# Loading the weights of the first expert pairs: down 0 issued without the wait for the gather, gate 2 loaded in two parts

## The chip, the cores and the metric

One core of a Trainium2 chip runs the kernel. The metric is the device time of one execution in microseconds (us), where less is better. One execution is also recorded by the hardware profiler; its trace is what the rows below are read from. Engines are named as the profile names them: PE is TensorE's matmuls, PEld its weight loads, DVE VectorE, ACT ScalarE, POOL GpSimd, SP SyncE. A "q" behind a name (SPq) is that engine's instruction queue, which waits on semaphores and issues DMAs.

## The reference

The reference is one inference step of a layer for 512 prompt rows and 64 sample rows of width 1024. First come three token mixers side by side (attention, a gated linear recurrence, a state-space scan), then a mixture of experts, then a last norm. The change touches only the start of the experts:

```python
def run_trunk(x, layer_params, g_final, past):
    ...
        mix, st = token_mixers(rmsnorm(h, lp['g_mix']), lp, layer_past)
        h = h + mix
        h = h + hier_moe(rmsnorm(h, lp['g_ffn']), ...)
    ...
def hier_moe(u, w_rg, b_rg, w_re, b_re, w_eg, w_eu, w_ed):
    ...
    def run_block(args):
        xb, e = args
        return (jax.nn.silu(xb @ w_eg[e]) * (xb @ w_eu[e])) @ w_ed[e]
```

Each of the 576 rows picks one of 4 groups, and in it 2 of 8 experts. An expert has three weight matrices in float32: gate and up (1024 x 512) and down (512 x 1024), 2 MB each. All 32 experts are computed, so 32 x 6 MB = 201 MB of weights are read in any case.

## The kernel before

The kernel is written out engine by engine: each engine has its own program, and semaphores order them. There is no scheduler; what stands first in an engine's program is issued first, and a wait holds up everything behind it on that engine.

The experts are worked through in 16 pairs. Pair i is experts i and i + 16, with 64 slots for rows each, so that a pair fills 128 partitions. For pair i:

- POOL issues a gather (an indirect DMA, in POOL's `expert_pair`) that fetches the pair's 128 rows of 4 KB from `u2d` in HBM into `xg`. Its landing counts in `xg_in`.
- PE turns the rows (`turn_rows`, 8 transposes), ACT and DVE copy them to `xT`.
- PE computes the gate product (`gate`, which calls `into`; 8 steps over the 1024 inputs, 2 experts each, and two PE instructions per float32 matmul, so 32 instructions), then the up product (`into` again, 32 instructions).
- ACT and DVE make silu(gate) * up, PE turns the result, and computes the down product (`down`, 32 instructions, in two halves of the columns). The end of the second half counts in `down_b`.
- PE later adds the result to the rows that it belongs to (`scatter`).

PE runs ahead: its `expert_pair(i)` does up i, turns the rows of pair i + 1, does gate i + 1, and then down i. So the order on PE at the start is gate 0, up 0, gate 1, down 0, up 1, gate 2, down 1, up 2, and so on.

The weights come by SP. `load(kind, i, first, second)` waits until the product that used the buffer before is done, and issues two DMAs of 2 MB, one per expert. There are two buffers for gate weights (`w_g[0]` for even pairs, `w_g[1]` for odd pairs), one for up (`w_u`), and one for down (`w_d`). So gate 2 must wait for the gate product of pair 0 (`gate_done`), up 1 for the up product of pair 0 (`up_done`), and down 1 for `down_b` of pair 0. Gate 0 is loaded during the mixers' last products; the rest starts when the last of these is done (`pj_full`). In the program of before, SP also waits for the first gather's landing before it issues down 0:

```python
            sp.wait_ge(S["xg_in"], 16)
            load("down", None, 0, EPAIRS)
            load("gate", 2, 2, 2 + EPAIRS, 0)
            load("up", 1, 1, 1 + EPAIRS)
            load("down", 1, 1, 1 + EPAIRS)
```

After this start, a loop issues up, gate and down of the pairs that follow, each with its wait. Below, "gate 2" or "down 1" means the weights, or the product, of that pair. The functions that the change touches:

Of the kernel before, what the change touches and what calls it, by code (L numbers as in the profile page):

```python
# [27 lines left out]
P = 128  # L28
# [6 lines left out]
KD = D // P  # L35
# [26 lines left out]
DE = D // 2  # L62
# [4 lines left out]
EPAIRS = NE // 2  # L67
# [216 lines left out]
def trunk_and_experts(nc, a, o):  # L284

    ctx = ExitStack()
    with ctx:
# [6 lines left out]
        def sem(name):  # L294
            return ctx.enter_context(nc.semaphore(name))
# [6 lines left out]
        def take(n):  # L302
            cut[0] += n
            assert cut[0] <= ARENA, cut[0]
            return cut[0] - n

        def at(off, *dims):
            n = 1
            for d in dims:
                n *= d  # L310
            v = arena[:, off:off + n]
            if len(dims) == 2:
                v = v.rearrange("p (a b) -> p a b", a=dims[0])
            if len(dims) == 3:
                v = v.rearrange("p (a b c) -> p a b c", a=dims[0], b=dims[1])
            return v

        def region(name, off, n, dt=F32R):

            return nc.alloc_sbuf_tensor_at(name, [P, n], dt, offset=arena_at + 4 * off)[:, :]
# [73 lines left out]
        first = region("first", cut[0], 2 * 2048, F32)  # L398
# [90 lines left out]
        rank, first, twice, place, col, side, is_over, div = (at(take(2 * NT), NT, 2) for _ in range(8))  # L489
# [14 lines left out]
        w_g = [at(wexp_off, 2 * KD, DE), at(take(2 * KD * DE), 2 * KD, DE)]  # L504
# [71 lines left out]
        def last_bank(k):  # L576
# [10 lines left out]
            lru_mu lru_h ob_r hs_ps hs_r td_r dec_ps acs_r d_r ea_r em_r e_r m_r xdt_r xdd_r tz_r mix_ps  # L587
            hcd_r h_r y0_r y1_r y2_r yg_r ssy_r vy_r sy_r yn_r yt_ps oc_r so_ps so_r so_out v_out tl_out
            tl_ps tl_r gm_r gains_in u2_r u2t_ps u2t_r lg_ps lg_r ids_r fexp_in fexp_r idx_r idx_seen over_c xg_in
            xt2_ps xt2_a xt2_d wu_in wd_in gate_done up_done gate_th gate_mul hid_r hidt_ps hidt_r down_a  # L590
            down_b yh_r yl_r hot_r sc_ps sc_r over_ps over_r fin_r fin_out dve_c pool_c sp_dve sp_act lru_pool side_dma""".split()
        S = {n: sem(n) for n in names}
        x_in = [sem(f"x_in{t}") for t in range(NT)]
        wg_in = [sem(f"wg_in{s}") for s in range(2)]
# [40 lines left out]
        def _(sp):  # L635
# [13 lines left out]
            for u, unit in enumerate(UNITS):  # L649
# [25 lines left out]
                else:  # L675
                    w = a[{"in": "w_in", "gate": "w_gate", "out": "w_out"}[unit[0]]]
# [5 lines left out]
            def load(kind, i, first, second, turn=0):  # L682

                name, dst, used, before, arrived = {
                    "gate": ("w_expert_gate", w_g[turn], "gate_done", 2, wg_in[turn]),
                    "up": ("w_expert_up", w_u, "up_done", 1, S["wu_in"]),
                    "down": ("w_expert_down", w_d, "down_b", 1, S["wd_in"])}[kind]
                if i is not None:
                    sp.wait_ge(S[used], i - before + 1)
                k = (DE if kind == "down" else D) // P  # L690
                for j, w in enumerate((first, second)):
                    half = dst[:, k * j:k * (j + 1), :].rearrange("p k f -> p (k f)").unsqueeze(1)
                    sp.dma_start(half, expert_w(name, w)).then_inc(arrived, 16)

            def expert_w(name, e):

                return a[name][0].rearrange("e (p k) f -> p e (k f)", p=P)[:, bass.ds(e, 1), :]
# [8 lines left out]

            load("up", None, 0, EPAIRS)
            load("gate", None, 1, 1 + EPAIRS, 1)

            sp.wait_ge(S["xg_in"], 16)  # L710
            load("down", None, 0, EPAIRS)
            load("gate", 2, 2, 2 + EPAIRS, 0)
            load("up", 1, 1, 1 + EPAIRS)
            load("down", 1, 1, 1 + EPAIRS)
            with sp.Fori(1, EPAIRS // 2 - 1) as ii:
                for turn in range(2):
                    i = 2 * ii + turn
# [31 lines left out]
        def _(pe):  # L749
# [4 lines left out]
            def params(_):  # L754
                pe.wait_ge(S["consts"], 7)
                pe.wait_ge(S["par_in"], 16 * (len(PAR_ROWS) + 2))
                pe.wait_ge(S["par_up"], 1)
                pe.transpose(ms[:, 0:NPAR], st_a[0:NPAR, :], ident[0:NPAR, 0:NPAR])
                pe.transpose(oa[:, 0:NST], st_b[0:NST, :], ident[0:NST, 0:NST]).then_inc(S["pe_par"], 1)
# [106 lines left out]
            def dt_turn(_):  # L866
                wait_drained(pe, IDX[("dt", 0, 1)])
                pe.wait_ge(S["ko_r"], NT)
                for t, (o0, n) in enumerate(TT):
                    m = pe.transpose(ms[0:n, t * 8:t * 8 + 8], dtT[0:8, o0:o0 + n], ident[0:8, 0:8])  # L870
                m.then_inc(S["dt_ps"], 1)
# [85 lines left out]
            def state_in(_):  # L957
                pe.wait_ge(S["lruw_in"], 16 * 5)
                pe.wait_ge(S["dt_raw"], 1)
                for j in range(WT):  # L960
                    m = pe.transpose(ms[:, j * P:(j + 1) * P], ss_in[:, j, :], ident)
                m.then_inc(S["hs_ps"], 1)
# [173 lines left out]
            def turn_rows(i, spare):  # L1136

                pe.wait_ge(S["xg_in"], (i + 1) * 16)
                for k in range(KD):
                    z = oa if k < KD // 2 else ms  # L1140
                    m = pe.transpose(z[:, (k % 4) * P:(k % 4 + 1) * P],  # L1141
                                     xg.rearrange("s (p k) -> s k p", k=KD)[:, k, :], ident)
                m.then_inc(S["xt2_ps"], 1)

            def into(i, b, w, spare, done):

                for k in range(KD):
                    for j in range(2):
                        m = pe.matmul(za[j * BLK:(j + 1) * BLK, b, :], xT[spare][:, k, j * BLK:(j + 1) * BLK],  # L1149
                                      w[:, j * KD + k, :], start=k == 0, stop=k == KD - 1)  # L1150
                m.then_inc(S[done], 1)

            def gate(i, turn, spare):
                par, n_turn = turn
                pe.wait_ge(S["xt2_a"], i + 1)
                pe.wait_ge(S["xt2_d"], i + 1)
                pe.wait_ge(wg_in[par], (n_turn + 1) * 32)
                into(i, 0, w_g[par], spare, "gate_done")

            def down(i, q, ks):  # L1160
                for k in ks:
# [7 lines left out]
            def expert_pair(i, spare, ahead=None, behind=2, over=None, last=False):  # L1169

                pe.wait_ge(S["wu_in"], (i + 1) * 32)
                into(i, 1, w_u, spare, "up_done")
                if ahead is not None:
                    if behind > 0:
                        pe.wait_ge(S["hidt_r"], i)
                    turn_rows(i + 1, 1 - spare)
                if behind > 0:
                    scatter(i - 1, range(6), behind > 1)
                if ahead is not None:

                    pe.wait_ge(S["gate_mul"], i + 1)
                    gate(i + 1, ahead, 1 - spare)
                pe.wait_ge(S["hid_r"], i + 1)
                for k in range(DE // P):
                    m = pe.transpose(oa[:, k * P:(k + 1) * P],
                                     hid.rearrange("s (p k) -> s k p", k=DE // P)[:, k, :], ident)
                m.then_inc(S["hidt_ps"], 1)
                if behind > 0:
                    scatter(i - 1, range(6, 2 * NT))
                    pe.wait_ge(S["sc_r"], 2 * NT * (i - 1) + 8)  # L1190
                pe.wait_ge(S["hidt_r"], i + 1)
                pe.wait_ge(S["wd_in"], (i + 1) * 32)
                if behind > 0 or over is not None:
                    pe.wait_ge(S["yl_r"], 2 * i)
                down(i, 0, range(DE // P))
                if last:
                    down(i, 1, range(DE // P // 2))
                    scatter_last(range(NT))
                    down(i, 1, range(DE // P // 2, DE // P))
                else:  # L1200
                    down(i, 1, range(DE // P))
# [47 lines left out]
                    item(n)  # L1249
            pe.wait_ge(S["routed"], 2)  # L1250
            turn_rows(0, 0)
            gate(0, (0, 0), 0)
            expert_pair(0, 0, ahead=(1, 0), behind=0)
            expert_pair(1, 1, ahead=(0, 1), behind=1)
            pe.wait_ge(S["routed"], 3)
# [6 lines left out]
            with ExitStack() as more:  # L1262
                for j in range(OPAIRS):
                    more.enter_context(pe.If(total > j))
                    i = EPAIRS + j
# [12 lines left out]
        def _(act):  # L1278
# [43 lines left out]
            def params(_):  # L1322
                act.wait_ge(S["par_in"], 16 * (len(PAR_ROWS) + 2))
                act.activation(w_dt_hr, w_dt, ACT.Copy).then_inc(S["wdt_r"], 1)
                act.wait_ge(S["pe_par"], 2)
                act.wait_ge(S["ut_u"], NT)
                act.activation(cpar, ms[:, 0:NPAR], ACT.Copy).then_inc(S["par_up"], 1)
                act.activation(cst, oa[:, 0:NST], ACT.Copy).then_inc(S["par_up"], 1)
# [120 lines left out]
            def state_in(_):  # L1449
                act.wait_ge(S["hs_ps"], 1)  # L1450
                act.activation(hS, ms[:, :], ACT.Copy).then_inc(S["hs_r"], 1)
# [1135 lines left out]
```

## Time and profile before

| | us |
|---|---|
| median of 3 runs | 1218.59 |
| lowest and highest run | 1214.49, 1219.43 |
| the profiled execution's own time | 1217.82 |
| its span in the trace, first to last instruction | 1216.0 |

The profiled execution's own time holds 1.8 us that lie around the span. All times of day below are us from the span's start. The mixers, the output projection and the routing take the first 713 us; the first gather is issued at 713.4, and the last pair's up weights land at 1174.8.

### The profile page before, as it was taken

What the parts mean: (1) busy time and instruction counts of PE and PEld (TensorE: products, weight loads), DVE (VectorE), ACT (ScalarE), POOL (GpSimd) and SP (SyncE); (2) the same over time, 40 slices, a digit from 0 to 9 for tenths busy, and PEclk for the clock granted to TensorE, in tenths of its full rate; (3) what the DMA queues carried; (4) which work ended last, traced back from release to release, by engine and by line L of the source; (5) the groups of instructions that cost most, each with busy time, mean ns of one, the idle gap of its engine ahead of it and who ended that gap; (6) DMA issues with size and microseconds to landing.
All of it is one profiled execution on the core that took longest, in us unless ns stands there. A gap on an engine that the chain in (4) does not pass through costs nothing.

```text
span 1216.0 us, 17138 instructions
## 1 busy us (share of the span) xinstructions
PE 1126.3 (93%) x6833; PEld 803.8 (66%) x6833; DVE 528.4 (43%) x992; ACT 381.4 (31%) x600; POOL 181.6 (15%) x196
## 2 busy tenths in 40 slices
PE   4999999999999999999999869999999999999994
PEld 4898777777988899999999853443433334343432
DVE  4331767763246465543444541332333323232336
ACT  3323676565547444433431101110111101010103
POOL 4000100211313346542310010000000000000000
PEclk8999999998999999999999859999999999999998
DMA  8279544363322212225263198999999999999982
GB/s 184 74 129 112 45 53 42 47 52 37 61 65 63 78 54 71 61 78 158 87 208 128 64 371 356 426 427 428 427 429 427 427 428 426 430 427 427 428 346 80
DMA packets 94316, 263.16 MB, mean 216 GB/s; under 512 B 5021, under 2 KB 75897, under 8 KB 81961
## 3 DMA queue, kind: packets, MB, share of 16 engines
q1 hardware_dynamic: 87664, 250.36, 61.0%
q0 software_dynamic: 3456, 6.58, 1.5%
q10 hardware_dynamic: 3128, 5.29, 1.2%
q8 instruction: 46, 0.75, 0.3%
q14 instruction: 22, 0.17, 0.0%
HBM read 258.24 MB, written 7.64 MB: 219 GB/s over the span
## 4 chain that ended last, share of the span: by engine, by line
PE 57%; DMA 26%; DVE 8%; ACT 5%; issue 3%; SPq 1%; DVEq 0%; POOLq 0%
DMA arena<-in_w_expert_up 23%; PE za L1149 12%; PE pj L777 11%; PE pj L778 10%; PE pj L779 10%; PE pj L804 2%; DMA ring<-in_w_in 2%; PE zb L1163 2%; DVE arena L1870 1%; DVE arena L1831 1%; DVE arena L1832 1%; ACT arena L1421 1%; ACT arena L1417 1%; PE ms L1076 1%; DVE arena L1845 1%
## 5 line engine op out<-in xcount | busy, mean ns | idle before, releaser
L1149 PE MATMUL za<-arena 128*64 128x512 f32 x1024 | 234.7, 613 | 23.6 <-DMA arena<-in_w_expert_up 21.8
L777 PE MATMUL pj<-u_high_r,ring_r 128*128 128x288 f32 x736 | 224.7, 305 | 0.5 <-ACT arena L1339 0.5
L778 PE MATMUL pj<-u_rest_r,ring_r 128*128 128x288 f32 x736 | 217.3, 295 | 0.0
L779 PE MATMUL pj<-u_high_r,ring_r 128*128 128x288 f32 x736 | 217.3, 295 | 0.0
L1149 PEld LDWEIGHTS za<-arena 128*64 128x64 f32 x1024 | 73.7, 141 | 176.0 <-issue 141.2
L777 PEld LDWEIGHTS pj<-u_high_r,ring_r 128*128 128x128 f32 x736 | 138.7, 189 | 13.4 <-issue 10.2
L778 PEld LDWEIGHTS pj<-u_rest_r,ring_r 128*128 128x128 f32 x736 | 138.8, 189 | 0.6
L779 PEld LDWEIGHTS pj<-u_high_r,ring_r 128*128 128x128 f32 x736 | 138.6, 188 | 0.0
L1710 DVE TENSOR_TENSOR ring_r<-ring,ring_r 128x1024 fp32r<-128x1024 f32 x62 | 78.5, 1271 | 105.5 <-ACT ring_r L1306 105.4
L1163 PE MATMUL zb<-arena 128*64 128x512 f32 x512 | 113.6, 595 | 3.9 <-DMA arena<-in_w_expert_down 1.5
L1163 PEld LDWEIGHTS zb<-arena 128*64 128x64 f32 x512 | 36.1, 137 | 74.3 <-issue 71.5
L1306 ACT ACTIVATE ring_r<-ring 128x1024 fp32r<-128x1024 f32 x62 | 64.5, 1051 | 20.6 <-DMA ring<-in_w_in 17.4
L2232 DVE SCALAR_TENSOR_TENSOR arena<-arena,za 128x512 f32<-128x512 f32 x16 | 11.0, 688 | 119.0 <-PE za L1149 119.0
L2248 DVE SCALAR_TENSOR_TENSOR y_rest<-zb,arena,y_high 128x512 fp32r<-128x512 f32 x32 | 24.0, 750 | 89.0 <-ACT y_high L1586 89.0
L1586 ACT ACTIVATE y_high<-zb,arena 128x512 fp32r<-128x512 f32 x32 | 22.0, 687 | 127.5 <-PE zb L1163 127.5
L2538 POOL COPY arena<-arena 128x1 int32 (+1 forms) x15 | 2.7, 182 | 382.1 <-PE ms L1141 382.1
L777 PE MATMUL pj<-ring_r,u_high_r 128*128 128x256 f32 (+1 forms) x160 | 48.4, 303 | 11.5 <-ACT arena L1342 4.8
L1383 ACT ACTIVATE arena<-pj,arena 128x288 f32<-128x288 f32 x48 | 24.0, 500 | 107.0 <-PE pj L779 106.9
L2204 DVE TENSOR_TENSOR arena<-arena,pj 128x512 f32<-128x512 f32 (+1 forms) x90 | 57.1, 674 | 0.0
L1567 ACT ACTIVATE arena<-oa 128x512 f32<-128x512 f32 x16 | 9.6, 600 | 150.0 <-PE ms L1141 150.0
L1570 ACT ACTIVATE arena<-za 128x512 f32<-128x512 f32 x16 | 9.6, 598 | 145.7 <-PE za L1149 145.7
L2226 DVE SCALAR_TENSOR_TENSOR arena<-arena,za 128x512 f32<-128x512 f32 x16 | 11.0, 689 | 101.3 <-ACT arena L1570 101.3
(441 smaller groups left out, 2082.3 us busy)
## 6 DMA issues: line engine op xcount, KB each, us to landing
arena<-in_w_expert_gate SPq DMA_DIRECT2D x32, 2048.0 KB, 26.3
arena<-in_w_expert_up SPq DMA_DIRECT2D x32, 2048.0 KB, 17.6
arena<-in_w_expert_down SPq DMA_DIRECT2D x32, 2048.0 KB, 16.7
ring<-in_w_in SPq DMA_DIRECT2D x26, 512.0 KB, 9.1
ring<-in_w_gate SPq DMA_DIRECT2D x24, 512.0 KB, 4.3
arena<-in_x_prompt SPq DMA_DIRECT2D x8, 512.0 KB, 8.8
ring<-in_w_branch_out SPq DMA_DIRECT2D x8, 512.0 KB, 3.4
ring<-in_w_in SPq DMA_DIRECT2D x2, 1024.0 KB, 15.7
```

What stands on the lines that cost most here:

```text
L777: pe.matmul(out, left[0], right[0], start=k == 0, stop=False)
L778: pe.matmul(out, left[0], right[1], start=False, stop=False)
L779: return pe.matmul(out, left[1], right[0], start=False, stop=k == last - 1)
L804: m = pe.matmul(bank[:, 0:HALF], ring4[s][:, k, m_cols], oAT[:, k, cols], start=k == 0, stop=k == WT - 1)
L1149: m = pe.matmul(za[j * BLK:(j + 1) * BLK, b, :], xT[spare][:, k, j * BLK:(j + 1) * BLK], w[:, j * KD + k, :], start=k == 0, stop=k == KD - 1)
L1163: m = pe.matmul(zb[j * BLK:(j + 1) * BLK, q, :], hidT[:, k, j * BLK:(j + 1) * BLK], w_d[:, j * (DE // P) + k, q * 512:(q + 1) * 512], star ...
L1306: act.activation(high_r[s], raw[s], ACT.Copy).then_inc(S["high_r"], 1)
L1383: m = act.activation(gsb[k % 2], bank[:, 0:HALF], ACT.Tanh, scale=0.5, bias=cpar[:, j:j + 1])
L1586: act.activation(y_high[:, half], zb[:, q, :], ACT.Copy, scale=weight_now).then_inc(S["yh_r"], 1)
L1710: dve.tensor_tensor(rest_r[s], raw[s], high_r[s], ALU.subtract).then_inc(S["rest_r"], 1)
L2204: dve.tensor_tensor(v, v, add_bank(k)[0:n, :], ALU.add).then_inc(S["sc_r"], 1)
L2248: dve.scalar_tensor_tensor(out=y_rest[:, half], in0=zb[:, q, :], scalar=weight_now, in1=y_high[:, half], op0=ALU.mult, op1=ALU.subtract).t ...
```

## The change

Three things are edited. SP issues down 0 right behind gate 1, with no wait for the gather. Gate 2 is no longer loaded by two DMAs (one per expert) behind the wait for the whole gate product 0, but by two DMAs that each carry half of the input rows of both experts: the first waits for a new semaphore `gate_rows`, the second for `gate_done`. And PE counts `gate_rows` up when four of the eight steps of gate product 0 are done. Nothing else differs; the bytes loaded are the same.

```diff
@@ SP's program
             load("up", None, 0, EPAIRS)
             load("gate", None, 1, 1 + EPAIRS, 1)
-
-            sp.wait_ge(S["xg_in"], 16)
             load("down", None, 0, EPAIRS)
-            load("gate", 2, 2, 2 + EPAIRS, 0)
+            for part, used in enumerate(("gate_rows", "gate_done")):
+                sp.wait_ge(S[used], 1)
+                run = slice(KD // 2 * DE * part, KD // 2 * DE * (part + 1))
+                sp.dma_start(w_g[0].rearrange("p (j k) f -> p j (k f)", j=2)[:, :, run],
+                             a["w_expert_gate"][0].rearrange("e (p k) f -> p e (k f)", p=P)[:, 2:3 + EPAIRS:EPAIRS, run]
+                             ).then_inc(wg_in[0], 16)
             load("up", 1, 1, 1 + EPAIRS)
@@ PE's program
-            def into(i, b, w, spare, done):
+            def into(i, b, w, spare, done, first=False):
                 for k in range(KD):
                     for j in range(2):
                         m = pe.matmul(za[j * BLK:(j + 1) * BLK, b, :], xT[spare][:, k, j * BLK:(j + 1) * BLK],
                                       w[:, j * KD + k, :], start=k == 0, stop=k == KD - 1)
+                    if first and k == KD // 2 - 1:
+                        m.then_inc(S["gate_rows"], 1)
                 m.then_inc(S[done], 1)
...
-            gate(0, (0, 0), 0)
+            gate(0, (0, 0), 0, first=True)
```

On SP, which issues all expert weights, these are the DMAs from up 0 to down 1 in the kernel before; each row is an issue, with the semaphore that it waits for:

```order
45 L693 DMA arena<-in_w_expert_up 128x4096 [waits pj_full]
46 L693 DMA arena<-in_w_expert_up 128x4096
47 L693 DMA arena<-in_w_expert_gate 128x4096 x2
48 L693 DMA arena<-in_w_expert_down 128x4096 [waits xg_in]
49 L693 DMA arena<-in_w_expert_down 128x4096
50 L693 DMA arena<-in_w_expert_gate 128x4096 [waits gate_done]
51 L693 DMA arena<-in_w_expert_gate 128x4096
52 L693 DMA arena<-in_w_expert_up 128x4096 [waits up_done]
53 L693 DMA arena<-in_w_expert_up 128x4096
54 L693 DMA arena<-in_w_expert_down 128x4096 [waits down_b]
55 L693 DMA arena<-in_w_expert_down 128x4096
```

And these are the same issues on SP in the changed kernel (line 713 is the new DMA of half the rows of gate 2):

```order
45 L693 DMA arena<-in_w_expert_up 128x4096 [waits pj_full]
46 L693 DMA arena<-in_w_expert_up 128x4096
47 L693 DMA arena<-in_w_expert_gate 128x4096 x2
48 L693 DMA arena<-in_w_expert_down 128x4096 x2
49 L713 DMA arena<-in_w_expert_gate 128x2x2048 [waits gate_rows]
50 L713 DMA arena<-in_w_expert_gate 128x2x2048 [waits gate_done]
51 L693 DMA arena<-in_w_expert_up 128x4096 [waits up_done]
52 L693 DMA arena<-in_w_expert_up 128x4096
53 L693 DMA arena<-in_w_expert_down 128x4096 [waits down_b]
54 L693 DMA arena<-in_w_expert_down 128x4096
```

The order of the loads is the same; down 0 has lost its wait, the first half of gate 2 has an earlier one, and up 1 and down 1 keep theirs. On PE the instructions of this stretch and their waits are the same in both kernels.

## Rows read from the trace of the kernel before

**Rows 1.** The page's chain that ended last: shares of the span by engine.
```profile
PE 57%; DMA 26%; DVE 8%; ACT 5%; issue 3%; SPq 1%; DVEq 0%; POOLq 0%
```

**Rows 2.** That chain in order of time, start and length in us, 712 to 760.
```profile
713.38 7.49 DMA arena<-u2d,arena
...
721.01 1.09 PE oa L1141 x4
...
723.85 15.60 PE za L1149 x64
739.45 0.64 PE oa L1141 x4
...
741.53 7.09 PE za L1149 x32
...
749.99 7.09 PE zb L1163 x32
```

**Rows 3.** The same chain from 1140 to the end.
```profile
1152.99 21.77 DMA arena<-in_w_expert_up
1174.81 7.09 PE za L1149 x32
```

**Rows 4.** Timeline of SP, 690 to 800: when each pair of loads was issued.
```profile
694.57 0.80 SPq L693 DMA_DIRECT2D arena<-in_w_expert_up  x2
...
720.89 0.80 SPq L693 DMA_DIRECT2D arena<-in_w_expert_down  x2
732.62 1.30 SPq L693 DMA_DIRECT2D arena<-in_w_expert_gate  x2
739.49 0.80 SPq L693 DMA_DIRECT2D arena<-in_w_expert_up  x2
757.11 0.80 SPq L693 DMA_DIRECT2D arena<-in_w_expert_down  x2
```

**Rows 5.** Stretches: length, busy time by engine, granted clock, DMA share, GB/s.
```profile
713.40:718.90 5.50, 4.42 (x20) 4.34 (x20) 0.84 (x5) 0.00 (x0) 1.08 (x1) 0.50 0.94 398
718.90:721.00 2.10, 0.03 (x1) 0.02 (x1) 0.18 (x1) 0.00 (x0) 0.00 (x0) 0.50 0.20 80
721.00:723.90 2.90, 1.99 (x10) 1.63 (x11) 0.80 (x3) 0.60 (x1) 0.18 (x1) 0.50 0.76 198
723.90:727.20 3.30, 3.30 (x8) 1.04 (x10) 2.59 (x9) 0.00 (x0) 1.03 (x1) 0.50 1.01 427
727.20:732.50 5.30, 5.30 (x28) 1.96 (x26) 0.00 (x0) 0.00 (x0) 0.00 (x0) 1.00 0.99 421
732.50:735.00 2.50, 2.50 (x15) 0.86 (x13) 0.69 (x1) 0.60 (x1) 0.00 (x0) 1.00 0.96 300
...
754.50:758.00 3.50, 3.50 (x18) 1.15 (x16) 0.82 (x2) 0.69 (x1) 0.00 (x0) 1.00 0.08 33
758.00:760.00 2.00, 2.00 (x12) 0.67 (x10) 0.59 (x1) 0.00 (x0) 0.00 (x0) 1.00 1.03 279
...
790.00:1174.00 384.00, 360.25 (x1640) 148.61 (x1636) 129.89 (x221) 41.25 (x65) 14.40 (x24) 0.98 1.00 423
```

**Rows 6.** The line of the gather: how long its 16 DMAs took from issue to landing.
```profile
DMA to landing us min/median/max: 7.5/10.8/11.3
```

**Rows 7.** DMA issues in 790 to 1174: count, KB each, median us to landing.
```profile
arena<-in_w_expert_gate SPq DMA_DIRECT2D x24, 2048.0 KB, 28.1
arena<-u2d,arena POOLq DMA_INDIRECT x12, 10.8
```

**Rows 8.** All waits of PE in 722 to 800: us in total, times, longest.
```profile
PE za L1149 <- DVE arena L2220: 1.0, 1, 1.0
PE za L1149 <- ACT arena L1567: 0.9, 1, 0.9
PE zb L1163 <- ACT arena L1576: 0.7, 1, 0.7
```

**Rows 9.** The longest wait of PE in 800 to 1175.
```profile
PE za L1149 <- DMA arena<-in_w_expert_up: 21.8, 13, 2.5
```

More of the change, by code:

```diff
@@ L589, in trunk_and_experts @@
             tl_ps tl_r gm_r gains_in u2_r u2t_ps u2t_r lg_ps lg_r ids_r fexp_in fexp_r idx_r idx_seen over_c xg_in
-            xt2_ps xt2_a xt2_d wu_in wd_in gate_done up_done gate_th gate_mul hid_r hidt_ps hidt_r down_a
+            xt2_ps xt2_a xt2_d wu_in wd_in gate_rows gate_done up_done gate_th gate_mul hid_r hidt_ps hidt_r down_a
             down_b yh_r yl_r hot_r sc_ps sc_r over_ps over_r fin_r fin_out dve_c pool_c sp_dve sp_act lru_pool side_dma""".split()
@@ L1150, in into, with gate @@
                                       w[:, j * KD + k, :], start=k == 0, stop=k == KD - 1)
+                    if first and k == KD // 2 - 1:
+                        m.then_inc(S["gate_rows"], 1)
                 m.then_inc(S[done], 1)
-            def gate(i, turn, spare):
+            def gate(i, turn, spare, first=False):
                 par, n_turn = turn
@@ L1157, in gate @@
                 pe.wait_ge(wg_in[par], (n_turn + 1) * 32)
-                into(i, 0, w_g[par], spare, "gate_done")
+                into(i, 0, w_g[par], spare, "gate_done", first)
             def down(i, q, ks):
```

## The prediction

> **What bounds the kernel now.** I read the chain that ended last first. By the page it is 57% PE and 26% DMA [rows 1], so the kernel is not one thing: the mixers are PE, the experts are weight loads. The second view is the end of that chain [rows 3]. There each step is an up load that takes over 20 us from issue to landing, then 7.1 us of the up product, then the next up load's issue. The stretches say why the loads take so long: from 790 to 1174 the DMA engines are fully busy at 423 GB/s [rows 5], and PE's longest wait there is for up weights, 21.8 us in 13 waits [rows 9]. So from about 760 to the end the loads run one behind the other with no gap, and the end moves exactly as far as the moment from which the loads never run dry. What happens before that moment counts only as far as it moves it.
>
> When is that? The stretches show three places after 713 where the DMA rate drops: 718.9 to 723.9 (80, then 198 GB/s), 732.5 to 735.0 (300), and 754.5 to 760.0 (33, then 279) [rows 5]. The timeline of SP [rows 4] says what each one waited for. In the first, up 0 and gate 1 have been moved and down 0 is issued at 720.89, behind the gather's landing. In the second, down 0 has been moved and gate 2 is issued at 732.62, behind gate product 0. In the third, up 1 has been moved and down 1 is issued at 757.11, behind the end of down product 0. The third is the last one, so the issue of down 1 is the moment that sets the end.
>
> What set that issue? The chain from 713 to 757 [rows 2]: the gather, 713.38 to 720.87; turning its rows from 721.01; gate and up product 0, 723.85 to 739.45; turning the next rows; gate product 1 from 741.53; down product 0 from 749.99, 7.09 us, ending at 757.08. After the gather no step of it waits for a weight load: PE's three waits from 722 to 800 are all for ACT or DVE, 0.7 to 1.0 us each [rows 8].
>
> **The change, part by part.** *Gate 2 in two parts, the first earlier.* The gate product 0 runs from 723.85 to about 732.6, where gate 2 is issued [rows 2, 4]. Half of its 32 instructions are 8 in 3.3 us at a granted clock of 0.50 and 8 more at full clock [rows 5], where one is 7.09/32 = 0.22 us [rows 2], so 3.3 + 1.8 = 5.1 us: `gate_rows` comes 3.6 us before `gate_done`. That starts 2.1 MB of loads earlier. But gate 2, up 1 and down 0 were all in time before [rows 8], and down 1 waits for PE. Whatever is saved in the first two gaps is waited for in the third. I cost this edit at 0. The cover is PE's chain, which lies behind it up to 757.08; without that cover the edit would give at most the second gap, (1 - 300/423) x 2.5 = 0.7 us. The added count on PE's matmul adds no instruction. Behind the new wait on SP's queue stand the second half of gate 2, up 1 and down 1, but each of them waits for a later product of PE anyway, so nobody waits longer.
>
> *Down 0 without the wait.* Its two issues cost SP 0.8 us at about 697 instead of at 720.89, with nothing behind them that could start earlier than `gate_rows`. Down product 0 needs the weights at 749.99 [rows 2], so their earlier landing is worth nothing to PE either. But 4.2 MB more now stand in the queue when the gather is issued at 713.38. Before, the first gather had a full DMA beside it only up to 718.9 (398 GB/s), then the engines to itself (80 GB/s from 718.9 to 721.0) [rows 5], and it landed after 7.49 us [rows 2]. That is the smallest of the 16 gathers; the median is 10.8 and the largest 11.3 [rows 6], and the twelve after 790, all under a full DMA, have a median of 10.8 too [rows 7]. In the changed kernel the first up load, gate 1 and down 0 follow one another, and down 0 alone lasts 4.19 MB / 423 GB/s = 9.9 us past 718.9, so to about 729: the gather is now like the others. I take 10.8, so +3.3 us; the bounds are 0 (7.5 again, the smallest) and +3.8 (11.3). A gain is excluded, since nothing that ran beside the gather is taken away.
>
> *What hangs on the gather.* POOL's next gather waits for the turned rows, so it is issued 3.3 us later too, at 727.4; PE needs it at 739.45 + 3.3 = 742.8 and even with 11.3 us it is there at 738.7. Turning, gate and up product 0 shift by 3.3. One term is open: before, the first 3.3 us of gate product 0 ran at a granted clock of 0.50 (1.2 GHz), after PE had been half idle since 718.9, and at 1.00 (2.4 GHz) from 727.2 on [rows 5]. If the clock rises as long after the product's start as before, this costs 0. The 8 instructions in those 3.3 us would take 1.8 at full clock, so a clock that is up from the start gives back 1.5 us, and one that rises 3.3 us later costs 1.5. PE's idle stretch ahead gets longer, which speaks against the gain; I take 0.
>
> *The loads after that.* The queue empties at 718.9 + 9.9 + 1.2 (the gather's 0.5 MB) = 730.0. The first part of gate 2 is issued at 727.15 + 5.1 = 732.2, so a gap is left there. Gate 2's 9.9 us then end at about 743.5 with the time to start; up 1 is issued at 742.8 and lands at about 754.6 with the next gather's 1.2 us. It is needed at 757.08 + 3.3 = 760.4. Down 1 is issued there, and the queue has been empty for some 6 us, where before it was for about 2.
>
> *The sum:* 0 for gate 2, +3.3 for the gather, 0 for the clock. The end shifts from 1216.0 to 1219.3 us of span, and with the 1.8 us around it from 1217.82 to **1221.1 us**. The median of the runs before, 1218.59, is 0.8 above the profiled execution; the forecast is 0.2% over that median. The three runs before lie 4.9 us apart (0.4%), so a difference under 0.5% can hardly be told from none.
>
> The Trainium skill has a rule that speaks the other way: "DMA: Bandwidth & Descriptors", section "Rules for kernel authors", says to issue a DMA early, to compute, and to wait for it late, because the fixed cost then overlaps. By that rule the early down 0 costs nothing and closes the first gap; the sum by it is that of the second rival below, and by the row of the gathers it is +3.3.
>
> **The rivals.** *The gather is not delayed* (1217.8): it could be that its first microseconds, not the load beside it, make its time. For it speaks that it was already under 398 GB/s for 5.5 of its 7.5 us [rows 5]; against it, that the twelve gathers that ran under a full DMA throughout have a median of 10.8 [rows 7].
>
> *The closed gaps reach the end* (faster). The gaps are (1 - 80/423) x 2.1 + (1 - 198/423) x 2.9 = 3.2 us and 0.7 us, so 3.9 us: 1213.9. It decides if down 1's issue is early by as much, that is, if PE's chain had waited for weights. Against it: it had not [rows 8]. Only if the third gap closed too, (1 - 33/423) x 3.5 + (1 - 279/423) x 2.0 = 3.9 us more, would it be 1210.
>
> *The clock rises later*: +3.3 + 1.5, 1222.6. For it: the longer idle stretch.
>
> *The gather stands behind all of down 0* (slower). Then it lands when down 0 has, at about 729 and its own last 1 to 2 us, so 9 to 10 us later than 720.87: about 1227. For it: the first gather before landed only when gate 1's load had ended. Against it: in steady state gathers land after 10.8 us while gate loads issued about the same time take 28.1 [rows 7], so they pass the loads that stand ahead. The Trainium skill says the same in "DMA: Bandwidth & Descriptors", section "Queues, rings and completion order": each engine takes turns between the queues that have work, packet by packet. By that rule this rival falls away.
>
> *The change does not do what it says* (1217.8): SP could be held at down 0's issue because too much stands in the queue. Against it: in the 28.1 us that a gate load took to land in the loop, 11.9 MB are moved at 423 GB/s [rows 5, 7], so almost six loads of 2.1 MB stood in the queue there, as many as up 0, gate 1 and down 0 make.
>
> **How the numbers follow.** Chances: the forecast 0.58, its own range 1219.5 to 1222.5 from the gather's bounds and half the clock's; gather not delayed 0.14; clock later 0.10; gaps reach the end 0.08; gather behind down 0 0.07; no effect 0.03. From 1217.8 to 1222.6 they hold 0.85 before the scatter of runs. The lowest run before lies 3.3 under the profiled one, the highest 1.6 above, so the range is 1214.5 to 1225. Faster than 1212.5 (0.5% under the median) only some of the closed gaps' case, 0.05; slower than 1224.7 the gather behind down 0 and a part of the later clock with scatter, 0.13; within, 0.82.
>
> **What would show it.** In the trace after: the first gather 10 to 11 us instead of 7.49; no DMA gap at 719 to 724, one at about 730 to 733 instead, and a longer one before down 1's issue, at about 760.4 instead of 757.11; gate product 0 starting at about 727; from there on every issue about 3.3 later. It is wrong if down 1 is issued before 757, if the gather lands before 722 or after 727, or if the loads after 790 do not run without gaps.

## The result, and the profile after

| | before | after |
|---|---|---|
| median, us | 1219.43 (20 runs) | 1222.94 (20 runs) |
| lowest and highest, us | 1214.49, 1221.41 | 1218.04, 1226.77 |
| span of the profiled execution, us | 1216.0 | 1221.1 |

The ratio is 1.0035, with a 95% interval of 1.0025 to 1.0046: the change costs 4.3 us (3.0 to 5.6). The ratio is worked out over all runs; the two medians alone lie 3.5 us apart. The prediction was 1221.1 us in a range from 1214.5 to 1225, with "within 0.5%" as by far the likeliest outcome. It holds, and in the direction that was forecast.

The chain of the changed kernel in order of time, start and length in us, answers to [rows 2]:

```profile
713.61 0.79 issue
714.40 11.69 DMA arena<-u2d,arena
...
726.23 1.09 PE oa L1144 x4
...
729.08 15.82 PE za L1152 x64
744.90 0.65 PE oa L1144 x4
...
746.97 7.09 PE za L1152 x32
...
755.43 7.09 PE zb L1168 x32
```

Line by line against [rows 2]: the gather takes 11.69 us instead of 7.49; gate and up product 0 take 15.82 instead of 15.60; everything else has the length that it had. The gather is issued 1.02 us later than before, at 714.40 instead of 713.38, but that is no effect of the change: up 0, the first load of the stretch, is already issued 1.03 us later (695.60, below, against 694.57 in [rows 4]), and nothing that was edited had run by then. The profiled executions differ so far by what happened in the mixers, so from here on times are counted from the gather's issue. From there to the end of the span it is 1221.1 - 714.40 = 506.7 us, where it was 1216.0 - 713.38 = 502.6: the loss of 4.1 us in this trace lies behind the gather's issue.

The timeline of SP in the changed kernel, with two issues to a row, answers to [rows 4]:

```profile
695.60 0.80 SPq L693 DMA_DIRECT2D arena<-in_w_expert_up  x2
696.44 1.10 SPq L693 DMA_DIRECT2D arena<-in_w_expert_gate  x2
697.59 0.98 SPq L693 DMA_DIRECT2D arena<-in_w_expert_down  x2
734.63 3.81 SPq L713 DMA_DIRECT2D arena<-in_w_expert_gate  x2
744.93 0.81 SPq L693 DMA_DIRECT2D arena<-in_w_expert_up  x2
762.55 0.80 SPq L693 DMA_DIRECT2D arena<-in_w_expert_down  x2
769.57 0.88 SPq L693 DMA_DIRECT2D arena<-in_w_expert_up  x2
```

Down 0 is issued 23 us earlier than before (697.59 instead of 720.89), and yet down 1 is issued 762.55 - 714.40 = 48.15 us after the gather, where it was 757.11 - 713.38 = 43.73. The difference is 4.4 us: 4.2 from the gather and 0.2 from product 0.

The stretches show the DMA side (length, busy time of PE, PEld, DVE, ACT and POOL, granted clock, DMA share, GB/s), and answer to [rows 5]:

```profile
718.90:721.00 2.10, 1.05 (x5) 0.94 (x5) 0.17 (x1) 0.00 (x0) 0.00 (x0) 0.50 1.04 433
721.00:723.90 2.90, 0.00 (x0) 0.00 (x0) 0.00 (x0) 0.00 (x0) 0.00 (x0) 0.50 0.97 412
...
728.00:730.00 2.00, 1.10 (x5) 0.37 (x6) 1.55 (x6) 0.60 (x1) 0.82 (x2) 0.50 0.77 328
730.00:732.00 2.00, 2.00 (x8) 0.76 (x6) 1.85 (x5) 0.00 (x0) 0.40 (x1) 0.50 0.45 109
732.00:734.00 2.00, 2.00 (x9) 0.59 (x7) 0.00 (x0) 0.00 (x0) 0.00 (x0) 0.78 0.29 113
734.00:736.00 2.00, 2.00 (x12) 0.77 (x10) 0.00 (x0) 0.00 (x0) 0.00 (x0) 1.00 0.31 53
736.00:740.00 4.00, 4.00 (x21) 1.41 (x19) 0.69 (x1) 0.60 (x1) 0.00 (x0) 1.00 0.92 334
...
758.00:764.00 6.00, 6.00 (x30) 2.01 (x28) 1.47 (x2) 1.37 (x2) 0.00 (x0) 1.00 0.26 55
...
790.00:1174.00 384.00, 359.65 (x1646) 148.85 (x1644) 129.95 (x220) 40.56 (x64) 14.45 (x24) 0.99 1.01 427
```

The gap at 719 to 724 is closed (433 and 412 GB/s where it was 80 and 198). The idle time comes back in the two gaps behind it, which are both longer than before: from 728 to 736, since the loads are through before half of gate product 0 is done, and from 758 to 764, before down 1. After 790 the loads run without gaps as before (427 GB/s; the 423 of [rows 5] takes in the end of the last loads, and up to 1140 it is 428 there).

All 16 gathers of the changed kernel, from issue to landing, answer to [rows 6]:

```profile
DMA to landing us min/median/max: 4.2/10.8/11.7
```

The largest is the first gather. The smallest, 4.2 us, is one that met almost idle engines: the second gather, issued at 729.37 into the gap that opens at 728. What the first gather moved is in the trace too (its queue, packets, MB, share of the engines, 714.9 to 726.1):

```profile
q0 software_dynamic: 144, 0.36, 8.1%
```

The kernel before shows the same 0.36 MB. It is less than the 0.5 MB that were counted for 128 rows of 4 KB ahead of the result: 0.36 MB is some 88 rows, and the program lets the gather pass over slots that hold none. The second gather moved 0.39 MB, and the twelve of [rows 7] moved 3.50 MB, 0.29 each.

### The profile page after: what moved, and what is told of

Its sections match the earlier page's. It is cut to its first block, busy times and chain, and to the rows that moved or that the text cites. A ratio compares the mean times of both kernels' runs of the same rounds, so it can differ in the third digit from the quotient of the medians.

```text
span 1221.1 us, 17138 instructions
## 1 busy us (share of the span) xinstructions
PE 1125.7 (92%) x6833; PEld 803.4 (66%) x6833; DVE 528.4 (43%) x992; ACT 381.5 (31%) x600; POOL 182.0 (15%) x196
## 4 chain that ended last, share of the span: by engine, by line
PE 56%; DMA 27%; DVE 8%; ACT 5%; issue 3%; SPq 1%; ACTq 0%; DVEq 0%; POOLq 0%
DMA arena<-in_w_expert_up 22%; PE za L1152 12%; PE pj L780 10%; PE pj L781 9%; PE pj L782 9%; DMA ring<-in_w_in 3%; PE pj L807 2%; PE zb L1168 2%; DVE arena L1875 1%; DVE arena L1836 1%; DVE arena L1837 1%; DMA arena<-u2d,arena 1%; ACT arena L1426 1%; ACT arena L1422 1%; DVE arena L1850 1%
```

## The experiments

The theory, called the gather theory below: the whole loss is the first gather, which now shares the DMA engines with down 0 until it has landed; PE's products and with them the next loads are late by as much, and nothing makes it up, since from then on the loads run without a gap. The rivals: the two-part load of gate 2 costs something; idle DMA time counts by itself, wherever it is.

All runs in one table. "Gather" is its time from issue to landing; the two columns behind it count from the gather's issue to the issue of down 1 and of up 2, from each run's timeline of SP; the ratio is to the kernel before, on the same chip, with its 95% interval.

| run | gather, us | to down 1 | to up 2 | ratio |
|---|---|---|---|---|
| before | 7.5 | 43.7 | 50.8 | |
| changed | 11.7 | 48.2 | 55.2 | 1.0035 (1.0025 to 1.0046) |
| e1 down 0 early, alone | 11.5 | 48.2 | 55.3 | 1.0032 (1.0021 to 1.0044) |
| e2 gate 2 in two parts, alone | 7.0 | 44.2 | 51.2 | 0.9993 (0.9982 to 1.0003) |
| e3 half of gate 1 late | 4.5 | 43.3 | 51.9 | 1.0003 (0.9993 to 1.0014) |
| e4 down 1 in halves | 7.8 | 40.9 | 51.3 | 0.9999 (0.9984 to 1.0015) |
| e7 down product 0 first | 7.3 | 36.9 | 50.9 | 1.0000 (0.9984 to 1.0015) |
| e8 changed kernel, down product 0 first | 11.3 | 40.1 | 54.0 | 1.0013 (0.9997 to 1.0030) |
| e9 as e7, gate 2 in two parts | 7.4 | 36.4 | 50.3 | 0.9994 (0.9980 to 1.0009) |
| e11 e9 once more | 7.9 | 37.4 | 51.2 | 0.9995 (0.9981 to 1.0009) |
| e10 as e9, a quarter of gate 1 late | 5.0 | 34.3 | 50.3 | 0.9977 (0.9964 to 0.9989) |

**e1: down 0 early, alone.** From the kernel before:

```diff
-            sp.wait_ge(S["xg_in"], 16)
             load("down", None, 0, EPAIRS)
```

> Only one half of the change: down 0 is issued without the wait for the gather; gate 2 is loaded whole, behind gate product 0, as before. The gather theory (the whole loss is the first gather sharing the DMA engines with down 0): the first gather takes 11 to 12 us instead of 7.5, the time from the gather's issue to down 1's issue is 48 us as in the changed kernel (43.7 before), and the time is 1.0035 of before, +4 us. The rival (the loss comes from the two-part load of gate 2): under +2 us.

Measured: 1.0032, and the chain has the same long gather:

```profile
712.45 11.47 DMA arena<-u2d,arena
...
726.90 16.03 PE za L1147 x64
```

This one edit gives the whole loss, so the two-part load is not needed for it. Of the 4.4 us that down 1 came later, 4.0 are the gather and 0.4 product 0 (16.03 us instead of 15.60). From the gather's issue to the end of the span it is 1219.5 - 712.45 = 507.0 us, as in the changed kernel.

**e2: gate 2 in two parts, alone.** The changed kernel with the wait for the gather back ahead of down 0:

```diff
             load("gate", None, 1, 1 + EPAIRS, 1)
+            sp.wait_ge(S["xg_in"], 16)
             load("down", None, 0, EPAIRS)
```

> The other half alone: gate 2 is loaded in two parts, the first behind gate_rows, and down 0 keeps its wait for the gather. Gather theory: the gather takes 7.5 us, the time from its issue to down 1's issue stays at 43.7, and the time is that of before, within 1 us; the second DMA gap gets shorter and the third longer by as much. The rival that the two-part load costs: +2 us or more. The rival that a closed gap brings its length: 0.7 to 2 us less.

Measured: 0.9993, an interval that holds 1. The first part was issued 728.87 - 712.57 = 16.3 us after the gather, where the whole gate 2 of before came after 19.2, but down 1 came after 44.2 as against 43.7: earlier loads, no earlier products. Product 0 took 1.0 us longer in this run, which used up the 0.5 us by which the gather was faster:

```profile
722.56 16.57 PE za L1153 x64
```

The rival of a cost of 2 us or more is out. The rival of a gain of 0.7 to 2 us is not out by the time, whose interval reaches from -2.2 to +0.4 us; in the trace nothing of such a gain is left at down 1's issue.

**e3: less beside the gather.** From the kernel before, the load of the second expert of gate 1 moved behind the wait:

```diff
-            load("gate", None, 1, 1 + EPAIRS, 1)
-            sp.wait_ge(S["xg_in"], 16)
+            for j, w in enumerate((1, 1 + EPAIRS)):
+                if j == 1:
+                    sp.wait_ge(S["xg_in"], 16)
+                half = w_g[1][:, KD * j:KD * (j + 1), :].rearrange("p k f -> p (k f)").unsqueeze(1)
+                sp.dma_start(half, expert_w("w_expert_gate", w)).then_inc(wg_in[1], 16)
             load("down", None, 0, EPAIRS)
```

> The opposite dose, from the kernel before: the load of the second expert of gate 1 is moved behind the wait for the gather as well, so that less runs beside the first gather. Gather theory: the gather takes about 6 us instead of 7.5, the time from its issue to down 1's issue falls from 43.7 to about 42.2, and the time falls by 1.5 us (0.9988), although the DMA engines now stand idle for some 6 us around the gather. The rival that idle DMA before 724 is what counts: 4 to 5 us more.

Measured: the gather was faster still than expected, 4.5 us, but the time did not fall (1.0003). The chain says where the 3 us went (start and length; L1227 is PE's last routing product):

```profile
716.64 4.47 PE zb L1227 x20
...
721.36 1.12 PE oa L1143 x4
...
724.23 16.94 PE za L1151 x64
...
741.56 18.59 DMA arena<-in_w_expert_up
...
760.19 4.94 PE za L1151 x21
```

The gather had landed at 715.54 + 4.5 = 720.0, but PE was in the routing product until 721.1, so only 1.8 of the 3 us reached the turning of the rows (5.8 us after the gather's issue instead of 7.6). Product 0 took 16.94 us, 1.3 more than before, and the granted clock stayed at 0.50 longer: it rose 6.0 us after the product's start, where before it had been 3.3 (727.2 in [rows 5]).

```profile
723.90:729.00 5.10, 4.77 (x12) 1.65 (x14) 2.93 (x11) 0.07 (x1) 1.03 (x1) 0.50 0.98 416
729.00:733.00 4.00, 4.00 (x18) 1.37 (x16) 0.00 (x0) 0.00 (x0) 0.00 (x0) 0.84 1.01 426
```

And up 1, pushed back by the idle DMA time, landed at 760.15 and had to be waited for (1.4 us). So the first step of the theory is confirmed in the other direction (less beside the gather, a faster gather), and the expected gain went into three things that stood right behind it: PE's routing product, the slower product 0, and the wait for up 1. The rival's 4 to 5 us of loss did not appear either.

**e4: down 1 in halves.** From the kernel before, the first half of down 1's columns is loaded when the first half of down product 0 is done (PE's wait counts the two extra DMAs):

```diff
-            load("down", 1, 1, 1 + EPAIRS)
+            for q, used in enumerate(("down_a", "down_b")):
+                sp.wait_ge(S[used], 1)
+                cols = slice(512 * q, 512 * (q + 1))
+                for j, w in enumerate((1, 1 + EPAIRS)):
+                    sp.dma_start(w_d[:, 4 * j:4 * (j + 1), cols],
+                                 a["w_expert_down"][0].rearrange("e (p k) f -> e p k f", p=P)[w][:, :, cols]
+                                 ).then_inc(S["wd_in"], 16)
```

> From the kernel before: down 1 is loaded in two column halves of both experts, the first as soon as the first half of down product 0 is done (its columns of the buffer are free then), the second behind down_b as before. If the issue of down 1 sets the end: it comes 3.5 us earlier after the gather's issue (40.2 instead of 43.7), the last DMA gap of 3.9 us shrinks to about 1, and the time falls by about 3 us (0.9975). If the end is not set there: no change within 1 us. The halves are rows of 2 KB instead of 16 KB; if these load slowly, some of the 3 us is lost.

Measured: down 1's first issue came at 40.9 us, near the expected 40.2, and the time was 0.9999. That is not the 3 us that were expected if down 1's issue sets the end; it is what was expected if the end is not set there. The stretches of this run show two things that took from the gain:

```profile
754.50:760.00 5.50, 5.50 (x28) 1.81 (x26) 1.50 (x2) 1.37 (x2) 0.00 (x0) 1.00 0.84 318
760.00:764.00 4.00, 4.00 (x22) 1.34 (x20) 0.00 (x0) 0.00 (x0) 0.00 (x0) 1.00 1.04 392
764.00:766.00 2.00, 2.00 (x14) 1.24 (x11) 0.77 (x2) 0.08 (x1) 0.00 (x0) 1.00 1.06 393
766.00:769.00 3.00, 3.00 (x14) 1.87 (x14) 3.00 (x6) 0.52 (x1) 1.19 (x2) 1.00 1.14 344
```

The gap at 754.5 to 760 is mostly filled (318 GB/s instead of 33 and 279), but rows of 2 KB move at 392 to 393 GB/s, and at 766 to 769 a new dip stands, worth 0.6 us against 423 GB/s: up 2, issued at 764.99, is the next load that comes when PE lets it.

**e7: down product 0 first.** This takes away one of the two, the slow rows. The loads stay as they are, with their rows of 16 KB; for pair 0 alone, PE, ACT and DVE do the down product before gate product 1. On PE:

```diff
-            expert_pair(0, 0, ahead=(1, 0), behind=0)
+            first_pair()
...
+            def first_pair():
+                pe.wait_ge(S["wu_in"], 32)
+                into(0, 1, w_u, 0, "up_done")
+                turn_rows(1, 1)
...
+                down(0, 0, range(DE // P))
+                down(0, 1, range(DE // P))
+                pe.wait_ge(S["gate_mul"], 1)
+                gate(1, (1, 0), 1)
```

> From the kernel before, with its loads and their waits as they were: for pair 0 alone PE does down product 0 before gate product 1 (ACT and DVE follow in the same order), so that the down buffer is free earlier. If the third DMA gap, before down 1, is what the end hangs on: down 1 is issued about 36 us after the gather instead of 43.7, up 2 as before after 50.7, the loads run without the third gap of 3.9 us, with rows of 16 KB unlike in the halves, and the time falls by 3 to 3.5 us (0.9973). If the end hangs on PE's chain to up 2's issue instead: within 1 us of before.

Measured: down 1 came at 36.9 us, up 2 at 50.9, and the time was 1.0000. The gap moved once more:

```profile
760.00:764.00 4.00, 4.00 (x22) 1.29 (x18) 0.00 (x0) 0.00 (x0) 0.00 (x0) 1.00 1.01 430
764.00:767.00 3.00, 3.00 (x18) 2.11 (x15) 1.82 (x3) 0.60 (x1) 0.18 (x1) 1.00 0.92 298
767.00:770.00 3.00, 3.00 (x15) 1.39 (x16) 3.00 (x6) 0.00 (x0) 1.01 (x1) 1.00 0.89 366
770.00:784.00 14.00, 13.93 (x68) 5.46 (x66) 4.49 (x9) 1.88 (x3) 0.00 (x0) 1.00 1.01 424
784.00:787.00 3.00, 3.00 (x18) 1.00 (x16) 0.75 (x1) 0.69 (x1) 0.00 (x0) 1.00 0.98 399
787.00:790.00 3.00, 3.00 (x18) 1.00 (x16) 0.00 (x0) 0.00 (x0) 0.00 (x0) 1.00 0.92 295
```

Against 423 GB/s, the dips from 764 to 770 (ahead of up 2, issued at 764.94) and from 784 to 790 (ahead of down 2, issued at 785.39) are worth 1.3 and 1.1 us, so at least 2.4 of the 3.9 us of the closed gap are lost again, and the rest is too little for the interval. In the kernel before there was no such dip: up 2 and down 2 came as late after the gather, but the loads ahead of them had started later. So down 1's issue is not the one place on which the end hangs. Down 1, up 2 and down 2 all hang on PE's chain from the first gather, and while that chain is late, closing one gap opens the next.

**e8 and e9: the new order with the change, and with its harmless half.** e8 is the changed kernel with e7's order; e9 is e2 with e7's order.

> The changed kernel with the same order on PE (down product 0 before gate product 1). Gather theory: the gather takes 11 to 12 us here too, everything on PE behind it comes 4 us later, up 2's issue too, and the time is 4 us over that of the run without the change (about 1.001 of before). The rival that the change loses only because down 1 had to wait for PE, and that its closed gaps count once down 1 is free earlier: the same as the run without the change or 2 to 4 us less.

> The order on PE as in the two others, gate 2 in two parts, and down 0 with its wait for the gather: what is left of the change without the part that delays the gather. Gather theory: the gather takes 7 to 7.5 us, and the time is that of the run with the new order alone, up to 1 us less, since up 2's issue then ends the wait. The rival that the second gap counts now: 1 to 2 us less than that run.

Measured: e8 1.0013, e9 0.9994. The gather takes 11.3 us in e8 and 7.4 in e9, and up 2 is issued 3.7 us later in e8. The two kernels differ in nothing but the wait ahead of down 0, and their 12 times each were taken on the same chip: the mean is 1219.7 us in e8 and 1216.5 in e9, so e8 is 3.2 us longer (1.1 to 5.2, from the scatter of the times). So in the new order, too, the early down 0 costs time. Against e7 (mean 1218.3) e8 is only 1.4 us longer (-0.5 to 3.3), and from the gather's issue to the end of the span it is 503.8 us in e8, 502.3 in e7, 500.2 in e9. The 4 us that the gather theory expected against e7 are not seen in full; of the rival, the 2 to 4 us of gain are out, but the same time as e7 is not. Whether in this order a part of the delay is made up by the closed gaps stays open, and so does whether e9 is faster than e7, as its rival said.

**e10 and e11: a quarter of gate 1 behind the gather.** e10 is e9 with gate 1 loaded as six eighths of the rows before the gather's wait and two eighths behind it; e11 is e9 once more.

```diff
-            load("gate", None, 1, 1 + EPAIRS, 1)
-            sp.wait_ge(S["xg_in"], 16)
+            for lo, hi in ((0, 6), (6, KD)):
+                if lo:
+                    sp.wait_ge(S["xg_in"], 16)
+                run = slice(DE * lo, DE * hi)
+                sp.dma_start(w_g[1].rearrange("p (j k) f -> p j (k f)", j=2)[:, :, run],
+                             a["w_expert_gate"][0].rearrange("e (p k) f -> p e (k f)", p=P)[:, 1:2 + EPAIRS:EPAIRS, run]
+                             ).then_inc(wg_in[1], 16)
             load("down", None, 0, EPAIRS)
```

> The version with gate 2 in two parts and down product 0 first, down 0 behind the gather, and in addition the last quarter of gate 1 (1 MB) behind the gather, so that less runs beside it. Gather theory: the gather takes 5 to 6 us instead of 7.3, PE turns its rows 1.5 to 1.9 us earlier after the gather's issue (PE's own product of the weights ends 5.6 us after it, so no earlier than that), up 2 is issued 48.5 to 49 us after the gather instead of 50.3, and the time is 1.5 us under that of the same version without the quarter. If idle DMA around the gather counts: 1 us over it. If the granted clock rises later after PE's start, up to 1.5 us of the gain is gone.

> The version with gate 2 in two parts and down product 0 first once more, beside the one with the quarter on the same chip, since its first time (0.9994, 0.998 to 1.0009) could not be told from that of before. By its first trace, where the last up weights landed 459.1 us after the gather's issue against 461.4 in the kernel before, it should be 2 us faster (0.998).

Measured: e10 0.9977, e11 0.9995. e10 is faster than the kernel before beyond its interval, by 2.8 us (1.3 to 4.4). In its trace the gather takes 5.0 us:

```profile
DMA to landing us min/median/max: 5.0/10.8/11.3
```

But the step behind it was not as expected: up 2 came 50.3 us after the gather, not 48.5 to 49, because PE now waited 1.9 us for up 1:

```profile
PE za L1158 <- DMA arena<-in_w_expert_up: 1.9, 1, 1.9
```

e11 missed its 2 us: 0.9995, though it is the kernel of e9; from the gather's issue to the end of the span the one trace of e9 has 500.2 us and that of e11 502.2, so one trace can lie 2 us from the next. Whether e10 beats e11 by the gather, or by how much, is not settled by these runs. The means are 1215.9 and 1217.7, 1.8 us apart (0.1 to 3.5, from the scatter of the times), which is the expected size at the edge of the noise; but the one trace of e10 shows the faster gather spent on that wait, and 501.7 us from the gather's issue to the end.

## Why the prediction was right

*What bounds it.* Right that the loads run without a gap from some moment, and that the end moves with that moment. Too narrow in naming down 1's issue as that moment: e4 and e7 move it by 3 and 7 us without a measurable gain. What the end follows is PE's chain from the first gather, of which down 1's issue is one link and up 2's the next. For the change the two say the same, since it shifts both by 4.4 us. The table's column to up 2 goes with the ratio better than the one to down 1: where up 2 is within 1.2 us of before, the time is that of before, and where it is 4.4 or 4.5 later, the time is 4 us longer. It does not do so everywhere: in e8 up 2 is 3.2 us later for 1.6 us of time (-0.4 to 3.7), and e10 is faster with no earlier up 2 than e9.

*Gate 2 in two parts: 0.* Right: e2, 0.9993, with what was saved in the first gaps waited for before down 1.

*Down 0 without the wait: 0 for itself, +3.3 by the gather.* The mechanism was right, by e1; the size was 0.9 too small. The gather took 11.69 us, 4.20 more than in [rows 2], and above the 11.3 that was taken as the largest of 16 [rows 6]. The row that it was read from, the gathers in the loop, is not quite its like: those moved 0.29 MB each, this one 0.36; whether the 0.9 us comes from that is not shown. The "0.5 MB" in the prediction's count of the queue is too much by the same reading, and its 1.2 us would be 0.9.

*The clock: 0, with 1.5 either way.* Here it cost at most 0.2 us (15.82 instead of 15.60). Over all runs product 0 took 15.27 us (e10) to 16.94 (e3), so the bounds were about right, and the term is real from one execution to the next.

*The loads after that.* The gap before down 1 came as forecast, but shorter than "some 6 us": up 1 was through within 758 to 759, so some 4 us stood empty up to the issue at 762.55.

```profile
758.00:759.00 1.00, 1.00 (x8) 0.37 (x6) 0.00 (x0) 0.00 (x0) 0.00 (x0) 1.00 0.23 98
759.00:762.50 3.50, 3.50 (x20) 1.21 (x18) 0.75 (x1) 0.69 (x1) 0.00 (x0) 1.00 0.00 0
```

The gap ahead of gate 2 was longer than the 2 us that were worked out: against 423 GB/s the four stretches from 728 to 736 are worth 5.2 us. Gate product 0 began 14.7 us after the gather's issue rather than 13.8, and after its first half's issue at 734.63 it took until 736 to 740 for the rate to come back (334 GB/s there). So gate 2 and up 1 were loaded later than forecast, and idle time moved from the next gap into this one.

*The rivals.* "Not delayed" and "the gather stands behind all of down 0" are out by the 11.7 us. "The closed gaps reach the end" is out: the first gap is closed in the trace, and the two behind it grew. "The clock rises later" is out with its 0.2 us, and "the change does not do what it says" with down 0's issue at 697.59.

*The number.* The sum was +3.3; measured, +4.3 (3.0 to 5.6). The forecast's own range, 1219.5 to 1222.5, just misses the median of 1222.94, and most of those 1.8 us above 1221.1 are no error of the sum: 1217.82, on which it stands, is one execution, and the 20 runs of the kernel before have a median 1.6 us higher. That the wide range holds is owed to its room for the scatter of runs. That "a difference under 0.5% can hardly be told from none" was too careful: with 20 runs of each, 0.35% stands clear of none.

The rule of the Trainium skill that spoke for the change ("DMA: Bandwidth & Descriptors", section "Rules for kernel authors": issue a DMA early and wait for it late) brought no time here: e1 does only that, and costs 0.32%. The trace agrees with the rule that the Trainium skill has on the same page, section "Queues, rings and completion order", that each DMA engine takes turns between its queues: the gather took 4.2 us beside next to nothing and 11.7 beside a full queue of loads, and it landed at 726.09, while loads that had been issued ahead of it still ran (328 GB/s from 728 to 730).

## What to carry to other kernels

Before a load is moved ahead, ask which small transfer then shares the engines with it, and what waits for that transfer: here 4.2 MB that nobody needed yet made a gather of 0.36 MB land 4 us later, and PE's whole chain with it. Where a stage's loads run back to back, a closed gap counts only if what frees the next buffers comes earlier too; count from the event that starts that chain to each of the next issues, and look for the gap at the following one. Profiled executions can differ by some us ahead of the change (the gather was issued at 710.5 in e9 and at 715.8 in e8), so measure intervals from an event, not times of day.

## What was not expected of the hardware

- The time of gathers of 0.3 to 0.4 MB went with what stood beside them: 4.2 us beside almost idle engines (the changed kernel's second gather), 4.5 with 2 MB held back (e3), 5.0 with 1 MB held back (e10), 7.0 to 7.9 with gate 1's tail beside it, 10.8 in the loop, 11.3 to 11.7 with down 0 beside it.
- Loads of rows of 2 KB moved at 392 to 393 GB/s (e4), loads of rows of 16 KB at 430 in the same place (e7).
- Product 0, the same 64 instructions, took between 15.27 and 16.94 us from run to run. The longer the granted clock stayed at 0.50 after its start, the longer it took: 2.7 us in e10 (15.27), 3.3 in the kernel before (15.60), 6.0 in e3 (16.94).
